# A two-block transformer kernel: mLSTM gates from folded weights, head statistics read from the banks, conformer chunks between the mLSTM chunks

## What is computed

```
p   = rmsnorm(x) @ w_in + b_in            # 6144 columns: xm, z, a, g, s, t
xc  = silu(conv4(xm))                     # causal, 4 taps, by channel
q,k = blockdiag(xc, wq), blockdiag(xc, wk)   # 256 blocks of 4 x 4
v   = blockdiag(xm, wv)
gates = concat(q, k, v) @ w_gate + b_gate    # 3072 x 8: 4 input, 4 forget gates
h   = mlstm(q, k, v, gates)               # 4 heads of 256, chunkwise, with a running maximum
h   = num / max(|den|, exp(-m));  hn = (h - mean(h)) * rsqrt(var(h) + 1e-5)
y_m = ((hn * norm_g + skip * xc) * silu(z)) @ w_down
u   = conv31(a * sigmoid(g));  y_c = silu(layernorm(u)) @ w_pw + b_pw
x  += (sigmoid(s) * y_m + sigmoid(t) * y_c) @ w_out
x  += cross_attention(rmsnorm(x), rmsnorm(mem));  x += conv_ffn(rmsnorm(x))
```

## Time and profile before

| | us |
|---|---|
| median of 3 runs (2680.24 to 2683.55) | 2683.18 |
| the profiled execution | 2681.67 |
| its span | 2679.9 |
| busy in the span: PE / PEld / DVE / ACT | 2612.3 / 2327.1 / 2187.2 / 1527.1 |
| second stack, layer 0 from its first chunk | 1549.9 |
| second stack, layer 1 from its first chunk | 2115.0 |

### The profile page before, as it was taken

One profiled execution on the slowest core, in us unless ns is written; L12 is line 12 of the kernel. 1 busy time (PEld: TensorE's weight loads), 2 busy tenths in 40 slices (PEclk: granted clock), 3 DMA queues, 4 the chain that ended last, 5 costly groups with the idle time before them and its releaser, 6 DMA issues.

```text
span 2679.9 us, 37969 instructions
## 1 busy us (share of the span) xinstructions
PE 2612.3 (97%) x15765; PEld 2327.1 (87%) x15765; DVE 2187.2 (82%) x2462; ACT 1527.1 (57%) x1581; POOL 48.4 (2%) x84
## 2 busy tenths in 40 slices
PE   7989999999999999999999999999999999999998
PEld 6879988878888888888888898998899999998998
DVE  6978877798989898898989889975577789954777
ACT  3533345577777777777777664544544555354554
POOL 1000000000000000000000000000000000000000
PEclk9999999999999999999999999999999999999999
DMA  9759964299999999999999863443555534454453
GB/s 321 236 209 374 353 214 159 78 382 387 365 354 360 354 360 350 365 353 358 360 346 361 293 197 126 150 162 126 192 189 189 177 111 134 158 177 154 166 184 114
DMA packets 376145, 669.87 MB, mean 250 GB/s; under 512 B 26777, under 2 KB 199583, under 8 KB 371103
## 3 DMA queue, kind: packets, MB, share of 16 engines
q1 hardware_dynamic: 358336, 662.02, 70.1%
q10 hardware_dynamic: 17631, 5.35, 0.8%
HBM read 663.13 MB, written 4.19 MB: 249 GB/s over the span
## 4 chain that ended last, share of the span: by engine, by line
PE 84%; DVE 10%; ACT 3%; DMA 2%; issue 1%; POOL 0%; ACTq 0%; SPq 0%; DVEq 0%; POOLq 0%
PE PS L447 24%; PE PS L449 24%; PE PS L448 24%; DVE LO L442 3%; DVE AR L2959 3%; PE PS L555 2%; PE PS L2667 2%; PE PS L1724 1%; ACT HI L433 1%; PE PS L2030 1%; PE PS L761 1%; DMA AR<-in_w_ada_dram 1%; PE PS L2706 1%; PE PS L2723 1%; PE PS L2542 1%
## 5 line engine op out<-in xcount | busy, mean ns | idle before, releaser
L442 DVE TENSOR_TENSOR LO<-RAW,HI 128x2048 fp32r<-128x2048 f32 x410 | 929.9, 2273 | 183.8 <-ACT HI L433 183.3
L433 ACT ACTIVATE HI<-RAW 128x2048 fp32r<-128x2048 f32 x410 | 780.4, 1904 | 343.3 <-PE PS L449 302.3
L447 PE MATMUL PS<-X1H,HI 128*128 128x256 f32 (+1 forms) x2128 | 610.0, 287 | 12.6 <-DVE X1L L635 6.6
L448 PE MATMUL PS<-X1L,HI 128*128 128x256 f32 (+1 forms) x2128 | 605.2, 284 | 0.0
L449 PE MATMUL PS<-X1H,LO 128*128 128x256 f32 (+1 forms) x2128 | 605.2, 284 | 0.0
L447 PEld LDWEIGHTS PS<-X1H,HI 128*128 128x128 f32 (+1 forms) x2128 | 409.4, 192 | 18.3 <-issue 15.8
L447 PE MATMUL PS<-HI,X1H 128*128 128x512 f32 x1056 | 419.7, 397 | 4.7 <-DVE LO L442 2.3
L449 PE MATMUL PS<-HI,X1L 128*128 128x512 f32 x1056 | 412.1, 390 | 0.0
L448 PE MATMUL PS<-LO,X1H 128*128 128x512 f32 x1056 | 411.5, 390 | 0.0
L448 PEld LDWEIGHTS PS<-X1L,HI 128*128 128x128 f32 (+1 forms) x2128 | 409.4, 192 | 1.8
L449 PEld LDWEIGHTS PS<-X1H,LO 128*128 128x128 f32 (+1 forms) x2128 | 409.3, 192 | 0.8
(11 more groups left out here) (399 smaller groups left out, 2818.6 us busy)
## 6 DMA issues: line engine op xcount, KB each, us to landing
RAW<-in_w_in_dram SPq DMA_DIRECT2D x66, 1024.0 KB, 5.4
RAW<-in_expert_w_gate_dram SPq DMA_DIRECT2D x66, 1024.0 KB, 6.9
RAW<-in_expert_w_up_dram SPq DMA_DIRECT2D x64, 1024.0 KB, 6.7
RAW<-in_expert_w_down_dram SPq DMA_DIRECT2D x62, 1024.0 KB, 6.4
RAW<-in_ffn_w_up_dram SPq DMA_DIRECT2D x55, 1024.0 KB, 5.7
AR<-in_expert_w_down_dram SPq DMA_DIRECT2D x50, 1024.0 KB, 6.9
AR<-in_expert_w_up_dram SPq DMA_DIRECT2D x48, 1024.0 KB, 6.3
AR<-in_expert_w_gate_dram SPq DMA_DIRECT2D x46, 1024.0 KB, 6.1
```

Source lines behind the costliest of these rows:

```text
L433: a.activation(HI[:, n % NH, 0:size(i)], raw_at(i), ACT.Copy).then_inc(*hi.up(i))
L442: v.tensor_tensor(LO[:, m % NH, 0:n], raw_at(i), HI[:, m % NH, 0:n].bitcast(F32), ALU.subtract).then_inc(*lo.up(i))
L447: t.matmul(o, lh, rh, start=first, stop=False)
L448: t.matmul(o, lh, rl, start=False, stop=False)
```

## The change

Five things.

1. The gate weights are folded ahead. In the expert stage 24 loads bring the gate weights of both layers, four partitions' copies of each group of rows, and six the 4 x 4 blocks (n = 8 to 37, one each). VectorE multiplies and adds them up (dve_fold, n = 40 to 47) into 64 columns for xc and 64 for xm a layer. `gates` then multiplies XM (all 8 chunks, behind the first value rows) and XC (behind g3) by them: 2 x 2 x 8 matmuls in place of 2 x 24.
2. The products for v, feature by feature, are gone; the value rows stay.
3. The order of TensorE's chunks is m0, m1, a0, g0, m2, m3, a1, and then as before; the stream of weights, the banks and the queues of ScalarE and VectorE follow. The k products stand behind the gate sum. The scores of a head wait for that head's k alone.
4. The conformer taps are spread otherwise on VectorE; one split_lo moves from before the gate sum to behind it.
5. The head statistics are taken from the banks. Mean and variance are corrected by the reciprocal denominators in small operations, and ScalarE makes one scaled copy of each piece behind the evacuation of s0.

Cut to its core, with the names of chunks and the calls of a queue shortened:

```diff
+ act_small (expert blocks 7 < n < 38):
+        l, j, i = m // 15, m % 15 // 4, m % 15 % 4
+        if j < 3:
...
+            a.dma_start(view(AR[i::4, WF_AT[l] + 32 * j:WF_AT[l] + 32 * j + 1], [96, 8], [1, 32]),
+                        AP(w.tensor, w.offset + 8 * 1024 * (3 * l + j), [[32, 32], [1024, 8], [1, 32]])).then_inc(
+                *small_in.up())
+    def dve_fold(v, m):      # expert blocks 39 < n < 48, m = n - 40
+        l, j = m // 4, m % 4
+        if m == 0:
+            v.wait_ge(*small_in.all())
+        if j < 3:
+            part = view(WF[l][:, 32 * j:32 * j + 1], [96, 8], [8, 4], [1, 8])
+            v.tensor_tensor(part, part, view(WB[:, 3 * l + j, :], [4, 8], [1, 4], [0, 8]), ALU.mult).then_inc(*dve_moe.up())
+        else:
...
+            v.tensor_reduce(view(U[:, WM(l, "c"):WM(l, "c") + 1], [8, 8], [1, 8]), view(WF[l][:, 0:1], [96, 8], [1, 8], [8, 8]),
+                            AX, ALU.add)
+            v.tensor_reduce(view(U[:, WM(l, "m"):WM(l, "m") + 1], [8, 8], [1, 8]), view(WF[l][:, 64:65], [96, 8], [1, 8], [8, 4]),
+                            AX, ALU.add).then_inc(*dve_moe.up("fold", l))
 pe_layer2:
+        def gates(part, src, off, first, last):
+            for k in range(2):
+                for c in range(8):
+                    o = WM(l, part) + 8 * c
+                    z = t.matmul(PS[:, 6 + k, 0:128], src[:, c, off + 128 * k:off + 128 * k + 128], U[:, o:o + 128],
+                                 start=first and c == 0, stop=last and c == 7)
-        for j in range(4):
-            chunk(f"in2{l}m", j, X1H, X1L, first=ready("n1") if j == 0 else None)
+        chunk(m0) chunk(m1)
         chunk(a0) chunk(g0)
+        chunk(m2) chunk(m3) chunk(a1)
         values_rows(0) values_rows(1)
-        chunk(a1) product(2, 0..1)
+        t.wait_ge(*dve_moe("fold", l))
+        gates("m", XM, 3, True, False)
         chunk(g1) values_rows(2) values_rows(3)
-        gates(2, range(4), True, False)
         chunk(a2)
-        product(2, 2..3)
         chunk(g2)
-        gates(2, range(4, 8), False, False)
         product(0, 0..1) chunk(a3) product(0, 2..3) chunk(g3)
+        gates("c", XC, 0, False, True)
         product(1, 0..3)
-        gates(0, range(8), False, False)
-        gates(1, range(8), False, True)
         for h in range(4):
+            t.wait_ge(*act_two("qkv", 1, h, l))
...
 act_layer2:
+        ev_m(0) ev_m(1)
         ev_a(0) ev_g(0)
-        ev_vt(0) ev_vt(1)
         first_taps(0)
+        ev_m(2) ev_m(3)
         ev_a(1)
-        ev_qkv(2, 0) ev_qkv(2, 1)
+        ev_vt(0) ev_vt(1)
...
             split_hi(a)        # behind ev_bias of s, j = 0
+            if j == 0:
+                a.wait_ge(*dve_two("heads", l))
+                for i in range(8):
+                    k, h = i // 4, i % 4
+                    z = a.activation(HT[:, k, 256 * h:256 * h + 256], PS[:, SB[h], 256 * k:256 * k + 256], ACT.Identity,
+                                     bias=HB8[:, i:i + 1], scale=HS8[:, i:i + 1])
 dve_layer2 (c = conv4, s = split_lo, T = conv_taps, G = glu):
-        c0 s c1 s c2 s c3 s s G0 s T20 s G1 T11 s T11 s T11 G2 s T12 s T11 G3 s T25
+        c0 s c1 s s G0 T6 s c2 T3 s c3 T4 s T15 s G1 T10 s T10 s T10 G2 s T10 s T10 G3
         gatesum, softplus
-          with T5 and T3 between, T19
+          with s T7 and T4 between, T14
...
             for k in range(2):
-                z = v.tensor_scalar(HT[:, k, 256 * h:256 * h + 256], PS[:, SB[h], 256 * k:256 * k + 256],
-                                    DN[:, 4 * k + h:4 * k + h + 1], None, ALU.mult)
-                z = v.bn_stats(ST8[:, 4 * k + h, :], HT[:, k, 256 * h:256 * h + 256])
+                z = v.bn_stats(ST8[:, 4 * k + h, :], PS[:, SB[h], 256 * k:256 * k + 256])
...
+        v.tensor_tensor(VR8, view(MV8[:, 1:2], [2, 8]), DN[:, 0:8], ALU.mult).then_inc(*dve_two.up())
+        v.tensor_tensor(VR8, VR8, DN[:, 0:8], ALU.mult).then_inc(*dve_two.up("hvar", l))
...
-            z = v.tensor_scalar(hv, hv, MV8[:, 2 * i:2 * i + 1], R8s[:, i:i + 1], ALU.subtract, ALU.mult)
+        v.tensor_tensor(HS8, R8s, DN[:, 0:8], ALU.mult).then_inc(*dve_two.up())
+        v.scalar_tensor_tensor(HB8, view(MV8, [2, 8]), -1.0, HS8, ALU.mult, ALU.mult).then_inc(*dve_two.up("heads", l))
```

More of the change, by code:

```diff
@@ L2544, in product @@
             z.then_inc(*pe_two.up("qkv", j, cp, l))
-        def gates(j, part, first, last):
+        def gates(part, src, off, first, last):
             for k in range(2):
[L2549 to L2552, removed]
-                                 U[:, o:o + 128], start=first and n == 0, stop=last and n == len(part) - 1)
-            z.then_inc(*pe_two.up("gates", j, part[-1], l))
+                for c in range(8):
+                    o = WM(l, part) + 8 * c
+                    z = t.matmul(PS[:, 6 + k, 0:128], src[:, c, off + 128 * k:off + 128 * k + 128], U[:, o:o + 128],
+                                 start=first and c == 0, stop=last and c == 7)
+            z.then_inc(*pe_two.up("gates", part, l))
         if l == 0:
@@ L2560, in pe_layer2 @@
         pe_to_fm(t, ("n1", l), XN, [4, 5, 6, 7], lambda nb: dve_two("normed", nb, "mix", l))
-        for j in range(4):
-            chunk(f"in2{l}m", j, X1H, X1L, first=ready("n1") if j == 0 else None)
+        chunk(f"in2{l}m", 0, X1H, X1L, first=ready("n1"))
+        chunk(f"in2{l}m", 1, X1H, X1L)
         chunk(f"in2{l}a", 0, X1H, X1L)
         chunk(f"in2{l}g", 0, X1H, X1L)
+        chunk(f"in2{l}m", 2, X1H, X1L)
+        chunk(f"in2{l}m", 3, X1H, X1L)
+        chunk(f"in2{l}a", 1, X1H, X1L)
         values_rows(0)
         values_rows(1)
-        chunk(f"in2{l}a", 1, X1H, X1L)
-        for cp in range(2):
-            product(2, cp, XM, 3, dve_two("bd", 2, l))
+        t.wait_ge(*dve_moe("fold", l))
+        gates("m", XM, 3, True, False)
         chunk(f"in2{l}g", 1, X1H, X1L)
@@ L2649, in pe_layer2 @@
         chunk(f"in2{l}s", 2, X1H, X1L)
-        t.wait_ge(*act_two("den", l))
-        t.wait_ge(*dve_two("heads", l))
+        t.wait_ge(*act_two("heads", l))
         pe_to_fm(t, ("ht", l), HT, FOUR)
@@ L2795, in act_layer2, with ev_m @@
         a.wait_ge(*pool_two("xmpad", l))
-        for j in range(4):
+        def ev_m(j):
             ev_bias(f"in2{l}m", j, XM, ACT.Identity, f"b_in{l}", 0, 3)
@@ L3335, in gpsimd_program2 @@
             g.wait_ge(*dve_two("hvar", l))
-            pool_rsqrt(g, R8s, view(MV8[:, 1:2], [2, 8]), LN_EPS, "heads", l)
+            pool_rsqrt(g, R8s, VR8, LN_EPS, "heads", l)
             g.wait_ge(*dve_two("utvar", 1, l))
```

114 lines of the change are left out of this document (59 added, 55 removed).

## The result

The changed kernel takes **2665.85 us** (median of five, 2665.56 to 2666.74), the kernel before 2682.28 us in as many runs beside it: a ratio of 0.9943, 95% interval 0.9932 to 0.9954, so 16.4 us or 0.6% faster. Its profiled execution took 2665.69 us with a span of 2663.9 us, against 2679.9 us of span before.

What follows compares the result with a forecast made beforehand. TensorE and VectorE were both taken as nearly full, the shorter saving counting: layer 0 -8.0 (VectorE), layer 1 -10.6 (TensorE), experts +0.5, together -18.1 us; from 2681.67 to 2663.6, plus 1.5 for the median: 2665.1 us, range 2660 to 2674.

Steps and rivals of the forecast that it cites:

- TensorE 7.0 us a layer less: In each layer, dropped value products save TensorE 3.46 us and the folded gate sum 3.58 us.
- All three stands of TensorE gone, 3.55 a layer: TensorE's waits before the third key product, the gate-sum turn and the running-maximum turn vanish, 3.55 us a layer.
- Layer 1, -10.6: VectorE ends its taps 5.4 us ahead there, so TensorE's whole saving counts: 10.6 us less.
- The clock piece of 1.5 us gone: Layer 0's half chunk after the maximum row, mostly at 1.2 GHz, returns to full clock, saving 1.5 us.
- Layer 0, -8.0: VectorE decides layer 0: 4.85 us less work plus 3.2 us fewer stands, so 8.0 us less.
- Stands of VectorE from 14.2 to 11 us by the new order: In layer 0, conformer chunks between mLSTM chunks let taps start sooner, cutting VectorE's idle time by 3.2 us.
- Folding, 0.5 us: In the expert stage, VectorE's folding products and reductions add 0.5 us to the path, bounds 0 and 4.6.
- A: Rival: TensorE decides both layers, 22.7 us less, 2660.5 us; chance 0.12.
- B: Rival: VectorE's stands don't shrink and TensorE's two gate stands return; 2670 to 2674 us; chance 0.12.
- C: Rival: ScalarE's wait for the first gated chunk reaches TensorE, 3.3 us a layer; 2671.7 us; chance 0.06.
- D: Rival: gate-weight loading in the expert stage, 6144 pieces of 128 bytes, makes it slower, 2705 us; chance 0.03.
- E: Rival: the change doesn't do what it says, for instance all waits reappear elsewhere; within 0.2%; chance 0.05.

Runs made afterwards that it cites:

- `pe_early`: Changed kernel plus sixteen spare matmuls of 128x256 on TensorE ahead of chunk a2 in both layers; 2676.37 us.
- `scan_first`: Changed kernel with VectorE's copy and scan of the gate row moved ahead of the split it queued behind; 2662.9 us.
- `undo_heads`: Changed kernel with the head statistics put back as before (scaled copies and normalising passes on VectorE); 2669.01 us.
- `undo_order`: Changed kernel with the first chunks put back in the order of before; 2661.28 us in a single run.
- `order_back`: Same kernel as `undo_order`, timed again in rounds beside the kernel before; median 2664.94 us, ratio 0.9949 to the kernel before.
- `fold_only`: Changed kernel with both head statistics and chunk order put back as before, leaving the folded gates alone; 2666.80 us.
- `combined`: Changed kernel with the scan ahead of the split, two splits behind the normalised rows, and folding four expert blocks later; median 2660.29 us, ratio 0.9930 to before.
- `fold_later`: Changed kernel with the expert stage's folding moved four expert blocks later; 2669.24 us, first to last SiLU of the experts 962.2 us.
- `taps_less`: Changed kernel with the last eight convolution taps left out in both layers; 2661.66 us.

## Why the prediction was right, and where it was not

The time, 2665.1 forecast and 2665.85 measured, and the case, my forecast's own, came out. That the time is so close is in part luck. The forecast drop was 18.1 us, and between the two profiled executions it was 16.0: layer 0 gave 0.6 less and layer 1 1.7 less, the experts cost 0.9 more, and the stage ahead of them, with the same code, gave 1.1 that I had not forecast. And I started from 2683.18, where the five runs beside the changed kernel have 2682.28.

- **TensorE 7.0 us a layer less: right in kind, 0.6 too small.** Between its own operations its work is 7.6 us less in each layer. With the stands (2.8 gone, 3.55 forecast) that makes 10.4, where I had 10.6: the two errors nearly cancelled. What the 0.6 is, beside the matmuls that I counted, no run took apart. Putting 6.9 us back near the same place costs 6.9 us in both layers (`pe_early`), so all of it counts.
- **All three stands of TensorE gone, 3.55 a layer: two of three.** The failed step is "The margin at the maximum row is about 1 us". I let ScalarE end z3's split in time, and did not see that the SiLU table would be loaded only behind the wait for chunk z0; that keeps 0.8 us in each layer. `scan_first` shows that it is only a matter of VectorE's order.
- **Layer 1, -10.6: right but for the clock.** The four profiles with an edit elsewhere and no piece there (`undo_heads`, `undo_order`, `order_back`, `fold_only`) have 231.1 to 231.3, which is -10.3; the changed kernel's two profiles have a piece and 232.6.
- **The clock piece of 1.5 us gone: wrong.** The failed step is "With the stands gone I take this 1.5 us as gone": one stand stayed, and so did the piece, which left layer 0 and appeared in layer 1. In the twelve profiles with the stand at the maximum row (24 layers) a piece lies behind it 11 times; in the two without it (`scan_first`, `combined`), never in four layers. That fits a tie to the stand, but four are too few to show it. The two conformer stands that came up in layer 0 bring pieces too (six profiles), hidden or not, and layer 1, which has no such stand, has none there. Which stand gets one differs between two profiles of one kernel (`undo_order`, `order_back`).
- **Layer 0, -8.0 (measured -7.4): the size by luck.** The failed step is "Which engine ends a layer's shared stretch is read at the turns of the conformer's output", taken for the whole layer. Up to the scan the layer goes at TensorE's pace, and 10.4 us came off there (110.9 to 100.5: 1665.1 - 1554.2 before); from the scan to the last tap it goes at VectorE's, and that grew by 3.1 us (101.1 to 104.2). VectorE had less time ahead of the scan, so it did 91.9 us of work there in place of 102.1; the other 10.2 us came to lie behind it, and less the 5.2 of the head statistics that is about what its busy time there shows, 95.7 before and 100.25 after. I had the sum from VectorE's queue instead: 4.85 for the statistics, of which 2.0 arrived, and 3.2 for the order, of which nothing did.
- **Stands of VectorE from 14.2 to 11 us by the new order: void.** They fell to 12.5 us (206.90 - 194.36), and not by the order, which leaves the time as it is. My walk found most of the new stands (first gated chunk 1.7, first taps 2.1 to 2.2, exponential 1.4 to 1.5). But a saving of stands ahead of a point where VectorE waits for others anyway is given back at that point.
- **Statistics from the banks, 0.5 us: too dear, 0.** One takes 416 ns from the banks, and 418 ns from SBUF in the kernel before. The Trainium skill ("VectorE: DVE Perf Modes", the section on the TRN2 errata) gives an operation on PSUM 62 cycles more; this trace doesn't show that for these statistics, and the measurement decides.
- **TensorE's 2.6 to 4 us left over in layer 0 as stands at its end: right in kind.** They are 2.5 and 2.2 us, where 0.3 stood before.
- **Folding, 0.5 us: 1.4 in the profile.** The failed step is "the most that a block gets is 1.1": with 1.83 us (1.18 + 0.65) for the two reductions, right behind VectorE's work on the expert's output, one block had more than its idle time: the expert boundaries lie 123.7 us apart, but the one around that block 125.1. `fold_later` gets 0.9 of it back.
- **Rivals.** A is out: TensorE does not decide the end of layer 0 (`taps_less`). B's mechanism came in part: of its two gate stands one, 0.8 of 2.0 us a layer, and VectorE's idle time shrank by 1.7 us, where I had 3.2 and B nothing. C did not come: TensorE stands for no bank at the first chunks. D is out: the experts cost 1.4 us more, most of it VectorE's. Its price was read from a row of other pieces (the earlier trace rows holds the 4 x 4 blocks, 0.05 MB in 3128 pieces, so 16 bytes each), but it holds for these too. With eight of the gate loads in the same window of the changed kernel, 760 to 960 us, a piece takes 0.017 x 16 x 200 / 5296 = 0.010 us in the mean. E is out: the waits did not all come back.

```profile
q1 hardware_dynamic: 29792, 70.48, 97.6%
q10 hardware_dynamic: 5296, 0.31, 1.7%
```

## What to carry to other kernels

Which engine bounds a stretch changes inside it: look for the points where the short engine waits for the long one (here the scan of the maximum row) and price each saving between two such points; ahead of one, a saving of the engine that waits there was worth nothing here. Order a queue so that what another engine waits for stands ahead of what is itself still waiting: one line moved gave 0.9 us a layer, two splits moved 2.4 us. Where single runs differ by a few us, cut the span at common operations; a gain of 0.9 us is plain in a stretch and invisible in the total.

## What the runs showed of the hardware that I had not expected

- The granted clock is at the lower level (1.2 GHz) for a short piece behind stands of TensorE, in one execution and not in the next: the same 11.9 us of work took 13.4 us. Ahead of the experts, where TensorE stands often, one code took 547.7 to 553.8 us, and the clock lost in the windows of the two ends is enough for the difference. Every piece in the two layers lies right behind a stand of TensorE of 0.8 to 2.7 us; which stand gets one, no run here could foretell.
- What a piece costs depends on the next stand. At the conformer's turns it cost nothing that shows where TensorE stood 2.2 us soon after (`undo_order`, `order_back`), and some 1.8 us where that stand was gone (`combined`).
- ScalarE's table load is not done ahead of the wait of the activation that needs it, although ScalarE is idle: it came after 6.3 us of standing, and its 1.28 us then were on the path to VectorE's scan.
- 6144 pieces of 128 bytes, loaded beside a weight stream that keeps the DMA engines full (97.6 to 98.1%), cost the expert stage at most 0.5 us more than the 6144 pieces of 32 bytes that the kernel before loads there, with the rest of the folding's own work in that figure.
